# A two-layer kernel on one core: the first stage by tiles of tokens, the values' weights first

## What is computed

```python
n = x * rsqrt(mean(x * x, axis=-1) + 1e-6) * g_mix
proj = n @ w_in                      # 1024 columns of n against queries, three pairs of keys and values, gates
b_gate, c_gate, h_conv, q, k_c, v_c, k_s, v_s, k_w, v_w, g_br, g_conv, g_attn = split(proj)
k_cmp, v_cmp = compress(k_c), compress(v_c)       # small MLP over blocks of 32 tokens
o = gates(g_br) . [attend(q, k_cmp, v_cmp), attend(q, k_s, v_s), attend(q, k_w, v_w)]
h = x + (sigmoid(g_conv) * conv(...) + sigmoid(g_attn) * (o @ w_attn_out)) @ w_o
h = h + (silu(norm(h) @ w_gate) * (norm(h) @ w_up)) @ w_down
# second block: differential attention with a relative bias, gated linear attention, pooling, a feed-forward
```

## Time and profile before

| | us |
|---|---|
| median of 3 runs | 745.41 (744.83 to 745.76) |
| profiled execution, its own time | 745.85 |
| its span, first to last instruction | 744.1 |
| TensorE busy in the span | 739.4 |
| VectorE, ScalarE, GpSimd busy | 517.9, 415.9, 66.5 |

### The profile page before, as it was taken

The page is one execution under the profiler, slowest core; times in us unless marked ns, Lnnn a source line. Parts: engine busy times, 40 slices in busy tenths (PEclk is TensorE's granted clock), DMA queues, the critical chain, the costliest instruction groups (busy, mean ns, idle before and its releaser), DMA issues.

```text
span 744.1 us, 11570 instructions
## 1 busy us (share of the span) xinstructions
PE 739.4 (99%) x4557; PEld 640.3 (86%) x4557; DVE 517.9 (70%) x834; ACT 415.9 (56%) x788; POOL 66.5 (9%) x103
## 2 busy tenths in 40 slices
PE   9999999999999999999999999999999999999998
PEld 8999989877788888888888888887888888888886
DVE  5784777795756677887367757898667777447762
ACT  6475557456454456565356547697646656346640
POOL 7300000000010000530000004400100000000000
PEclk9999999999999999999999999999999999999999
DMA  8998454343355546656655562735355655656511
GB/s 261 296 316 270 94 116 147 113 151 114 133 170 197 182 150 219 201 211 227 190 174 203 170 226 60 253 117 179 109 166 170 195 200 175 221 169 193 203 57 56
DMA packets 99209, 131.26 MB, mean 176 GB/s; under 512 B 5357, under 2 KB 79163, under 8 KB 99156
## 3 DMA queue, kind: packets, MB, share of 16 engines
q1 hardware_dynamic: 96564, 125.58, 52.5%
q0 software_dynamic: 2304, 4.43, 2.7%
q10 hardware_dynamic: 288, 0.52, 0.2%
HBM read 128.68 MB, written 1.84 MB: 175 GB/s over the span
## 4 chain that ended last, share of the span: by engine, by line
PE 97%; DVE 2%; ACT 1%; issue 0%; POOL 0%; POOLq 0%
PE B L1631 39%; PE B L1597 22%; PE B L1602 11%; PE B L1586 11%; PE B L1812 2%; PE B L1859 2%; PE B L1822 2%; PE B L1644 1%; PE B L1695 1%; DVE LO L1007 1%; PE B L1638 1%; PE B L1815 1%; PE B L1839 1%; PE B L1740 1%; PE B L1798 0%; PE B L1739 0%
## 5 line engine op out<-in xcount | busy, mean ns | idle before, releaser
L1007 DVE TENSOR_TENSOR LO<-RAW,HI 128x1024 fp32r<-128x1024 f32 x236 | 282.4, 1235 | 100.7 <-ACT HI L543 100.2
L1631 PE MATMUL B<-HI,AA 128*128 128x512 f32 (+1 forms) x960 | 286.4, 376 | 0.3 <-DVE AA L1013 0.2
L543 ACT ACTIVATE HI<-RAW 128x1024 fp32r<-128x1024 f32 (+1 forms) x240 | 236.9, 1038 | 61.4 <-PE B L1631 57.8
L1631 PEld LDWEIGHTS B<-HI,AA 128*128 128x128 f32 x960 | 175.7, 188 | 33.0 <-issue 1.1
L1597 PE MATMUL B<-AA,HI 128*128 128x512 f32 x704 | 179.2, 393 | 0.0
L1631 PE MATMUL B<-LO,AA 128*128 128x512 f32 (+1 forms) x480 | 178.5, 372 | 0.0
L1597 PEld LDWEIGHTS B<-AA,HI 128*128 128x128 f32 x704 | 126.7, 189 | 23.0 <-issue 0.7
L1631 PEld LDWEIGHTS B<-LO,AA 128*128 128x128 f32 x480 | 90.6, 189 | 14.7
L1602 PEld LDWEIGHTS B<-AA,LO 128*128 128x128 f32 x704 | 96.6, 190 | 7.1
L1602 PE MATMUL B<-AA,LO 128*128 128x256 f32 x704 | 98.8, 282 | 0.0
L1586 PE MATMUL B<-AA,HI 128*128 128x256 f32 x448 | 83.1, 286 | 0.0
(11 more groups left out here) (313 smaller groups left out, 634.1 us busy)
## 6 DMA issues: line engine op xcount, KB each, us to landing
RAW<-in_w_in SPq DMA_DIRECT2D x29, 1024.0 KB, 5.5
RAW<-in_w_gate SPq DMA_DIRECT2D x22, 1024.0 KB, 5.4
RAW<-in_w_up SPq DMA_DIRECT2D x22, 1024.0 KB, 5.4
RAW<-in_w_down SPq DMA_DIRECT2D x22, 1024.0 KB, 5.0
RAW<-in_w_in SPq DMA_DIRECT2D x10, 512.0 KB, 6.3
RAW<-in_w_attn_out SPq DMA_DIRECT2D x4, 1024.0 KB, 5.1
RAW<-in_w_o SPq DMA_DIRECT2D x4, 1024.0 KB, 5.0
RAW<-in_w_out SPq DMA_DIRECT2D x4, 1024.0 KB, 5.0
```

Source lines behind the costliest of these rows:

```text
L543: e.activation(pieces(HI, NSPL, i, k), pieces(RAW, NRAW, i, k), ACT.Copy).then_inc(split_hi, 1)
L1007: e.tensor_tensor(pieces(LO, NSPL, i, k), pieces(RAW, NRAW, i, k), pieces(HI, NSPL, i, k), ALU.subtract).then_inc(split_lo, 1)
L1631: x = e.matmul(dst, a, w[:, t, c0:c0 + n], start=(first and t == 0 and k == 0), stop=(last and t == nk - 1 and k == 2))
```

## The change

- **Transfers.** Both pieces of tile 0 are issued first, one on ScalarE's queue, one on SyncE's; tile 1's two pieces follow on ScalarE's, the gain row on SyncE's.
- **Norm by tiles.** Each tile has its own mean and its own power on GpSimd, tile 0 first. GpSimd's transfers of the small rows now stand behind both powers.
- **Turns.** x is multiplied by the gain alone. The root goes onto the diagonal of a 128x128 matrix (`root_turner`, from the identity), and a turn is an fp32 product of a piece of x with that diagonal, so it transposes and scales in one. Two instructions take the place of each transpose. ScalarE and VectorE no longer scale x.
- **First weights.** The selected values' weights become unit 0 and their products are issued in twelve quarters (tile, half of the contraction, which of the three parts), between the turns. The keys' unit follows, whole; units 0 to 11 of before move back by one. The values' products just before attention are gone.
- **Filler.** The products of ones go from 14, 3, 7 and 3 to 9, 1 and 3; the relative bias's product moves to behind the third turn.
- **Start of attention.** The first item of `fill` (half 0 of the window keys, its eviction ahead of the first exponents) is issued before the first scores. The bias transfer waits for the last query in place of the values.
- Semaphore values of the later roots and set-up steps are renumbered.

The diff, cut to its core:

```diff
+        cols(w1, KO + 768, 256, vals_pe, 2)
         cols(w1, KO + 512, 256, keys_pe, 2)
         cols(w1, KO, 256, block_pe, 2)
         cols(w1, KO + 256, 256, block_pe, 4)
         cols(w1, GBO, 48, gates_pe, 1)
-        U_Q, U_HID = (4, 7, 10, 11), (5, 8)
+        U_Q, U_HID = (5, 8, 11, 12), (6, 9)
...
-        cols(w1, KO + 768, 256, vals_pe, 2)
         cols(w1, KO + 1024, 256, keys_pe, 4)
...
-        U_KEYS, U_BLOCK, U_GATES, U_VALS = 0, 1, 3, 12
+        U_VALS, U_KEYS, U_BLOCK, U_GATES = 0, 1, 2, 4
...
-            for h in range(2):
-                e.dma_start(X[:, 0, halves(h)], A["x"][0, 0:128, halves(h)]).then_inc(x_in[h], 16)
-                if h == 0:
-                    e.dma_start(GAIN[0:128:64, :], A["g_mix"][0, :].rearrange("(a n) -> a n", a=2)).then_inc(row_in, 16)
+            e.dma_start(X[:, 0, halves(1)], A["x"][0, 0:128, halves(1)]).then_inc(x_in[1], 16)
+            e.dma_start(GAIN[0:128:64, :], A["g_mix"][0, :].rearrange("(a n) -> a n", a=2)).then_inc(row_in, 16)
             for i, (src, nk, n, _, _) in enumerate(units):
...
-            e.memset(REL[32:33, :], NEG).then_inc(far_set, 1)
+            e.memset(REL[32:33, :], NEG).then_inc(setup, 1)
+            e.wait_ge(setup, FAR)
+            root(1, ST[:, 6:7], ST[:, 4:5], 1)
+            e.wait_ge(root_sb, 1)
+            root(2, ST[:, 7:8], ST[:, 5:6], 1)
             e.dma_start(VR[0:12, :], A["conv_w"][0].rearrange("k (c p) -> (k c) p", p=128)).then_inc(rows_in, 16)
...
             e.dma_start(VR[46:47, :], A["gla_gate_b_2"]).then_inc(rows_in, 16)
-            e.wait_ge(far_set, 1)
-            root(1, ST[:, 6:8], ST[:, 4:6])
             for i, n in ((47, "q_norm_g_2"), (48, "k_norm_g_2"), (50, "gla_norm_g_2")):
                 for a in range(2):
...
-            e.wait_ge(vals_sb, 2)
+            e.wait_ge(q_sb, 8)
             e.dma_start(bias_rows.rearrange("h r n -> h (r n)").rearrange("h (r n) -> h r n", n=ROW),
...
+            e.dma_start(X[:, 0, halves(0)], A["x"][0, 0:128, halves(0)]).then_inc(x_in[0], 16)
             for h in range(2):
                 e.dma_start(X[:, 1, halves(h)], A["x"][0, 128:256, halves(h)]).then_inc(x_in[2 + h], 16)
...
+            def squares(col, src, scrap, h, done=squares_sb, by=1):
...
                 e.activation(scrap[:, halves(h)], src[:, halves(h)], ACT.Square, scale=1.0 / 32,
-                             accum_out=ST[:, col + h:col + h + 1]).then_inc(squares_sb, 1)
-
-            for t, h in ((0, 0), (1, 0), (0, 1)):
-                e.wait_ge(x_in[2 * t + h], 16)
-                squares(2 * t, X[:, t, :], QK[:, t, :], h)
+                             accum_out=ST[:, col + h:col + h + 1]).then_inc(done, by)
+
+            e.wait_ge(x_in[0], 16)
+            squares(0, X[:, 0, :], QK[:, 0, :], 0, squares0_sb)
+            e.wait_ge(x_in[2], 16)
+            squares(2, X[:, 1, :], QK[:, 1, :], 0, squares_sb, 3)
+            e.wait_ge(x_in[3], 16)
+            squares(2, X[:, 1, :], QK[:, 1, :], 1)
+            turned(0, B[5], 0, 0)
             hi(0, 0)
-            e.wait_ge(root_sb, 1)
-            for h in range(2):
-                e.wait_ge(gained_sb, 2 + h)
-                e.activation(TOK[:, 1, halves(h)], TOK[:, 1, halves(h)], ACT.Copy, scale=ST[:, 7:8]).then_inc(scaled_act, 1)
-                if h == 0:
-                    for t in range(2):
-                        turned(t, B[5 + t], 0, t)
+            turned(1, B[6], 4, 0)
             hi(0, 1)
-            for t in range(2):
-                turned(2 + t, B[5 + t], 4, t)
+            turned(2, B[5], 0, 1)
+            turned(3, B[6], 4, 1)
             hi(1)
...
+            values(0, 0)
+            hi(2)
+            values(0, 1)
             e.wait_ge(rel_pe, 1)
             e.activation(OH[0:4, :], B[4][0:4, 0:ROW], ACT.Copy).then_inc(rel_sb, 1)
             keys(0, 0)
-            hi(2, 0)
+            hi(3, 0)
             keys(0, 1)
-            hi(2, 1)
-            hi(3)
...
-            hi(U_VALS + 2)
...
-            values(0, 0)
-            values(0, 1)
...
             filler = fill()
+            next(filler)
             for i in range(NSTEP + 2):
                 if i < NSTEP:
                     exponents(i)
-                for _ in range(FILL_AT[i]):
+                for _ in range(FILL_AT[i] - (i == 0)):
                     next(filler)
...
+            def mean(t):
+                return e.scalar_tensor_tensor(ST[:, 4 + t:5 + t], ST[:, 2 * t:2 * t + 1], EPS, ST[:, 2 * t + 1:2 * t + 2],
+                                              ALU.add, ALU.add)
...
             def gained(t, h):
                 e.wait_ge(x_in[2 * t + h], 16)
-                e.tensor_tensor(TOK[:, t, halves(h)], X[:, t, halves(h)], B[2 + h][:, :], ALU.mult).then_inc(gained_sb, 1)
-
+                e.tensor_tensor(TOK[:, t, halves(h)], X[:, t, halves(h)], B[2 + h][:, :], ALU.mult).then_inc(scaled_sb, 1)
+
+            def root_turner(t):
+
+                e.wait_ge(root_sb, t + 1)
+                e.tensor_scalar(PT[:, t, 0:128], ident[:, :], ST[:, 6 + t:7 + t], None, ALU.mult).then_inc(root_diag, 1)
+
+            e.wait_ge(x_in[1], 16)
+            e.scalar_tensor_tensor(QK[:, 0, halves(1)], X[:, 0, halves(1)], 1.0 / 1024, X[:, 0, halves(1)], ALU.mult, ALU.mult,
+                                   accum_out=ST[:, 1:2]).then_inc(squares0_sb, 1)
+            e.wait_ge(squares0_sb, 2)
+            mean(0).then_inc(mean_sb, 1)
+            e.wait_ge(gain_pe, 1)
             gained(0, 0)
-            e.wait_ge(x_in[3], 16)
-            e.scalar_tensor_tensor(QK[:, 1, halves(1)], X[:, 1, halves(1)], 1.0 / 1024, X[:, 1, halves(1)], ALU.mult, ALU.mult,
-                                   accum_out=ST[:, 3:4]).then_inc(squares_sb, 1)
+            e.wait_ge(setup, IDENT)
+            root_turner(0)
+            gained(0, 1)
             e.wait_ge(squares_sb, 4)
-            e.scalar_tensor_tensor(ST[:, 4:6], ST[:, 0:4:2], EPS, ST[:, 1:4:2], ALU.add, ALU.add).then_inc(mean_sb, 1)
+            mean(1).then_inc(mean_sb, 1)
             gained(1, 0)
-            e.wait_ge(root_sb, 1)
-            e.wait_ge(gained_sb, 1)
-            e.tensor_scalar(TOK[:, 0, halves(0)], TOK[:, 0, halves(0)], ST[:, 6:7], None, ALU.mult).then_inc(scaled_sb, 2)
+            turned(0, B[5], 0, 0)
+            root_turner(1)
             gained(1, 1)
-            e.scalar_tensor_tensor(TOK[:, 0, halves(1)], X[:, 0, halves(1)], ST[:, 6:7], B[3][:, :], ALU.mult,
-                                   ALU.mult).then_inc(scaled_sb, 2)
             lo(0, 0)
-            for t in range(2):
-                turned(t, B[5 + t], 0, t)
+            turned(1, B[6], 4, 0)
             lo(0, 1)
-            for t in range(2):
-                turned(2 + t, B[5 + t], 4, t)
+            turned(2, B[5], 0, 1)
+            turned(3, B[6], 4, 1)
             lo(1)
+            lo(2)
             e.wait_ge(rows_pe, 1)
             e.tensor_copy(VT[:, 0:51], B[5][:, 0:51]).then_inc(rows_sb, 1)
-            lo(2)
+            lo(3)
...
-            lo(13)
-            lo(U_VALS + 2)
+            lo(14)
...
-            idle(14)
+            idle(9)
             e.wait_ge(row_in, 16)
             for h in range(2):
                 take(2 + h, scaled_sb, 4)
                 x = e.matmul(B[2 + h][:, :], ones[64 * h:64 * h + 1, :], GAIN[64 * h:64 * h + 1, :], start=True, stop=True)
             x.then_inc(gain_pe, 1)
-            idle(3)
-            e.wait_ge(rel_in, 32)
-            e.wait_ge(far_set, 1)
-            take(4, rel_sb, 1)
-            e.matmul(B[4][0:4, 0:ROW], REL[:, :], OH[:, :], start=True, stop=True).then_inc(rel_pe, 1)
-            idle(7)
-            e.wait_ge(setup, IDENT)
-
-            def turns(h):
-                e.wait_ge(scaled_sb, 2 * h + 2)
-                turn(2 * h, TOK[:, 0, halves(h)], 5)
-                e.wait_ge(scaled_act, h + 1)
-                turn(2 * h + 1, TOK[:, 1, halves(h)], 6)
+            idle(1)
+
+            def first_turn(n):
+
+
+                t, h = n // 2, n % 2
+                e.wait_ge(scaled_sb, n + 1)
+                e.wait_ge(root_diag, t + 1)
+                take(5 + h, turn_lo, n + 1)
+                for j in range(4):
+                    x = e.matmul(B[5 + h][:, 128 * j:128 * j + 128], TOK[:, t, 512 * h + 128 * j:512 * h + 128 * j + 128],
+                                 PT[:, t, 0:128], start=True, stop=True)
+                x.then_inc(turn_pe, 1)
...
+            hi, lo = view(HI, U_VALS), view(LO, U_VALS)
+
+            def quarter(t, h, a, w, first=False, last=False):
+
+
+                d = slice(t * 128, t * 128 + 128)
+                for c in range(4 * h, 4 * h + 4):
+                    x = e.matmul(B[t][:, 0:256], a[:, c, d], w[:, c, :], start=(first and c == 0), stop=(last and c == 7))
+                return x
+
+            first_turn(0)
+            first_turn(1)
+            idle(3)
+            take(0, vals_sb, 1)
+            e.wait_ge(split_hi, 1)
+            e.wait_ge(turn_hi, 1)
```

(68 more changed lines are left out.)

76 lines of the change are left out of this document (38 added, 38 removed).

## The result

| | runs | median us | lowest to highest |
|---|---|---|---|
| before | 12 | 745.59 | 744.83 to 746.47 |
| after | 12 | 747.27 | 746.09 to 749.28 |

The ratio is 1.0026, with a 95% interval of 1.0019 to 1.0034: slower, by 1.7 us. The forecast of 744.4 us missed by 2.9 us, and the range (to 745.9) didn't hold the time. The kernel was run again beside the first experiments: 747.78 us, ratio 1.0031 [1.0019, 1.0043] in 5 runs. The profiled execution took 746.96 us, its span 745.2 against 744.1 before.

What follows compares the result with a forecast made beforehand. TensorE, busy 99% of the span, was taken as the bound. Both unit products would end at 25.0 instead of 25.97 us, 1.0 less: 745.85 to 744.8, less 0.44 for the median, 744.4 us; range 743.4 to 745.9.

Steps and rivals of the forecast that it cites:

- the landmark: First stage: the end of both unit products (keys' and values') together, forecast at 25.0 us against 25.97 before.
- The path up to the first weight product: Start of the kernel: tile 0's norm, gain product, diagonal, first turn and high part, first weight product at 10.6 us against 13.14.
- The supply of weights up to the bias transfer: Weight transfers in the stretch to 75 us: supply close to demand, gaining 1.4 us, costed at nothing.
- the move of GpSimd's rows: Small-row transfers behind both roots: landed by 21 us, asked for at about 25.0, cover about 4 us, no cost.
- the pulled key: Start of attention: 2.88 us of a later key's products, moved ahead of the scores, cover the last query's eviction; no cost.
- three signs of being wrong: Gain product starting after 6 us, first turns at half rate, or a TensorE gap over 0.5 us between 11 and 85 us.
- the second part: Gain product behind shorter filler: starts at 5.2 us, ends at 6.9, with TensorE's clock doubling from about 6.4 us.
- The clock rises late: Rival, first stage: half rate lasts, each further us costs 0.5; chance 0.15 ending near the old time, 0.08 clearly slower.
- Against: they are short: Argument against the late-clock rival: TensorE's gaps around the gain product are short, and earlier filler reached full rate after 5.3 us.
- The 14.4 us from the first weight product to the landmark: TensorE from 10.6 to 25.0 us: 96 products 11.52, turns 2 and 3 1.8, bias product 0.73, one wait 0.35.
- the wait behind turn 3: First stage: turn 3's eviction must precede tile 1's second quarter, a wait of 0.2 to 0.4 us, taken as 0.35.
- no wait ahead of the first turn of weights: Start of attention: the first turn of attention weights, near 83 us before, keeps 2.0 us spare, so TensorE does not wait.

Runs made afterwards that it cites:

- e8: The changed kernel with the first item of `fill` put back behind the first attention scores: 749.46 us.
- e4: The changed kernel run and profiled once more, with nothing changed: 747.78 us, ratio to before 1.0031.
- e1: The changed kernel with ScalarE's second values' eviction moved ahead of the high part of unit 2 (`hi(2)`): 746.14 us.
- e10: e9 with the changed kernel's shorter filler (9 products ahead of the gain product and 1 behind, instead of 14 and 3): 746.4 us.
- e6: The changed kernel reordered: second values' eviction before `hi(2)`, bias product replacing turn 1's three fillers, tile 0's low-weight quarter before the quarter awaiting turn 3's eviction: 745.53 us.
- e12: The changed kernel with only its turns changed, to transposes of x already multiplied by root and gain in one VectorE instruction: 745.8 us.
- e7: The changed kernel with e5 and e6 together, the first diagonal made before the gain multiply and the first high part before turn 0's eviction: 745.26 us.
- e3: The changed kernel with three filler products instead of one between the gain product and the first turn: 746.14 us.
- e5: The changed kernel with before's filler around the gain product, 14 products ahead and 3 behind instead of 9 and 1: 747.03 us.
- e9: e7 with turns as transposes again, x multiplied by root and gain in one VectorE instruction: 744.15 us, ratio to before 0.9982.

## Why the prediction was wrong

**What held.** The bound and the landmark: in twelve of fourteen kernels the span is 718.0 to 718.4 us plus landmark plus later waits. The path up to the first weight product: gain row by 5.25 us (5.2 forecast), root 0 at 6.5 (6.7), first weight product 10.49 (10.6). The supply of weights up to the bias transfer, the move of GpSimd's rows (their transpose starts without a wait at 26.34 us) and the pulled key cost nothing, the last as e8 shows. Of the three signs of being wrong that it named, two came: first turns at half rate (e4, e1), and a gap over 0.5 us between 11 and 85 us (0.9 us at 20.48).

**The step that failed** is in the second part, "I read that as 1.2 GHz first and 2.4 GHz from about 6.4 us on", and what the sum made of it: a gain product and turns at the higher rate for good. The rows of before showed the rise of one execution whose filler ran without a pause to 7.02 us. The change takes away ten instructions ahead of the gain product and leaves pauses of 0.35 to 0.66 us ahead of the first turn. Of 17 executions two kept the rate, one of them profiled, and perhaps a third (747.12 us, mean clock 1.0). In eight the mean clock of 0.997 or 0.998 says that it fell back, as the profiled one of them shows (0.50 in e4). Six lie where the profiles of e1 and e8, by their spacing, have a late rise; none of those six was profiled, so this is inferred from the level. The rival "The clock rises late" named the cause and had 0.23; together with the fall, which it did not name, the executions gave it 14 or 15 of 17. Its first weight product, about 11.8 us, was too early: e1's is at 13.04, because turn 1 and the three filler products stand ahead of it on TensorE at half rate too (from 8.35 us), where the reckoning had turn 0 and ScalarE alone. Its price of 0.5 us for each further us at half rate is on the high side: e1's landmark is 28.38, 2.85 above that of the first profile less its bank wait (25.53), for a rise at about 13.5 in place of 5.8 us, or 0.37 us for each (an estimate). "Against: they are short" was the error: the clock fell in e4 with no pause longer than 0.66 us. The Trainium skill's rule that the moment of the rise differs from run to run (TensorE: Matmul & The Clock Gate, Part 1) is borne out, but the Trainium skill has a spread of half a microsecond there, and here the rise came from before 5.1 us (e4's gain product at full rate) to some 17.5 (e10), with the same short filler. That a clock once up comes down again inside the first 10 us is shown by the windows of e4, e6 and e12.

**The term that was missed.** The 14.4 us from the first weight product to the landmark were 15.92 (26.41 - 10.49). The turns (1.8 forecast, 0.99 and 0.81), the bias product (0.73) and the wait behind turn 3 (0.35 forecast, about 0.45) are right. The missing piece is 0.9 us of the keys' waiting for the values' bank behind `hi(2)`; e1 takes it out and gains 0.9 to 1.4 in the three groups. The remaining 0.5 is what 0.12 us a product leaves out at the ends of groups: four products behind another kind of work take 0.58 us from start to start (13.27 to 13.85) in place of 0.48. I counted TensorE's banks for the turns and not for the two units. Even where the rate rose early and stayed, the kernel would not have been faster than before: the low group stands at 746.09 and 746.96.

**The wait at 119.8 us** (0.5) was not foreseen either: "no wait ahead of the first turn of weights" was right and looked too near. It shows in after, e6, e7 and e10, where the unit took 28.5 us and more to land and ScalarE waited 2.9 to 3.1 us for it, and not in e1, e3, e4, e5, e9 and e12, with 27.8 or 27.9 us and 2.2 or 2.3. Before had 30.6 and 2.2, so it goes with ScalarE's wait and not with the landing alone. What makes the difference of 0.7 us was not tried and stays open, and so is how often it comes in other executions.

From 744.4 to 747.27, then: about 0.9 to 1.0 for the bank (shown by e1), 0.85 for the fallen clock of the middle group (e4 against the first profile), 0.1 for the wait behind turn 3, up to 0.5 for the late wait, and some 0.4 of ends of groups, less the 0.1 by which the first weight product came early. The sum is 2.3 to 2.8, and before itself had a median 0.2 us above the one that I started from. The high group adds its own: without it the median would lie lower.

**What the change was worth.** The order of the work (values first, by quarters, norm by tiles, pulled key) gains, but only together with the repairs: with the waits out, the filler back and transposes for turns it gives 744.15, 1.3 us under before, and no run has the order alone. The turns by products lose about 1 us (e9 against e7: 1.1, with befores that differ by 0.25) to 1.5 (e12 against after), and the shorter filler 2.25 (e10 against e9).
